# A one-core block: the order of the first transfers, the squares of x, and twenty warm-up matmuls

## The reference

```python
def rms_norm(x, w):
    xf = x.astype(jnp.float32)
    return (xf * lax.rsqrt(jnp.mean(xf * xf, axis=-1, keepdims=True) + RMS_EPS)).astype(x.dtype) * w

    u = rms_norm(h, norm_w[i])          # h = x for the first layer
    proj = u @ in_w                     # z | x, B, C | dt
    xbc = jax.nn.silu(causal_depthwise_conv(xbc, conv_w, conv_b))
    dt = jax.nn.softplus(dt_raw + dt_bias)
```

## Time and profile before

| | us |
|---|---|
| median of three runs | 927.24 |
| the profiled execution | 923.9 |
| its span, first to last instruction | 922.1 |
| PE busy | 874.7 (95%) |
| PEld busy | 841.7 (91%) |
| DVE busy | 553.8 (60%) |
| ACT busy | 481.3 (52%) |
| POOL busy | 620.7 (67%) |

### The profile page before, as it was taken

How to read it: one execution, slowest core, us unless ns; L and a number is a source line. 1 busy time by engine, 2 the same in 40 slices (tenths; PEclk the granted TensorE clock), 3 DMA queues, 4 the chain that set the end, 5 groups by cost and what they waited for, 6 DMA issues and landing times.

```text
span 922.1 us, 18225 instructions
## 1 busy us (share of the span) xinstructions
PE 874.7 (95%) x7019; PEld 841.7 (91%) x7019; DVE 553.8 (60%) x1553; ACT 481.3 (52%) x921; POOL 620.7 (67%) x274
## 2 busy tenths in 40 slices
PE   7999899998998799999999997989999999999995
PEld 6999899988997699999999986978999999999995
DVE  5998557773244744445358987666546666651165
ACT  6755555554455366555545465645555444544451
POOL 3899645556886355455869897343586888888980
PEclk9999899999999999999999998999999999999997
DMA  8677532323664334244646565332465666666621
GB/s 322 180 216 219 163 99 90 96 86 112 188 193 134 106 96 133 92 121 129 197 149 195 171 206 184 91 93 69 108 180 155 195 191 189 185 167 182 204 89 47
DMA packets 38534, 138.85 MB, mean 151 GB/s; under 512 B 4272, under 2 KB 4272, under 8 KB 38448
## 3 DMA queue, kind: packets, MB, share of 16 engines
q1 hardware_dynamic: 38448, 137.69, 49.6%
HBM read 136.63 MB, written 1.05 MB: 149 GB/s over the span
## 4 chain that ended last, share of the span: by engine, by line
PE 74%; DVE 6%; POOL 4%; ACT 2%; issue 2%; DVEq 0%; ACTq 0%
PE ps L548 20%; PE ps L549 19%; PE ps L550 19%; POOL wl L509 4%; PE ps L573 1%; PE ps L743 1%; PE ps L745 1%; PE ps L581 1%; PE ps L659 1%; PE ps L765 1%; PE ps L864 1%; DVE qr L1669 1%; ACT wh L980 1%; PE ps L641 1%; PE ps L888 1%
## 5 line engine op out<-in xcount | busy, mean ns | idle before, releaser
L509 POOL TENSOR_TENSOR wl<-raw,wh 128x1024 fp32r<-128x1024 f32 x254 | 609.3, 2420 | 260.5 <-ACT wh L980 260.4
L548 PE MATMUL ps<-uh,wh 128*128 128x256 f32 x1248 | 354.3, 284 | 7.3 <-DVE ul L1476 3.2
L549 PE MATMUL ps<-ul,wh 128*128 128x256 f32 x1248 | 349.7, 280 | 0.0
L550 PE MATMUL ps<-uh,wl 128*128 128x256 f32 x1248 | 349.4, 280 | 0.0
L980 ACT ACTIVATE wh<-raw 128x1024 fp32r<-128x1024 f32 x256 | 263.0, 1054 | 118.9 <-PE ps L550 115.6
L548 PEld LDWEIGHTS ps<-uh,wh 128*128 128x128 f32 x1248 | 236.1, 189 | 12.3 <-DVE ul L1476 3.4
L549 PEld LDWEIGHTS ps<-ul,wh 128*128 128x128 f32 x1248 | 235.9, 189 | 0.0
L550 PEld LDWEIGHTS ps<-uh,wl 128*128 128x128 f32 x1248 | 235.5, 189 | 0.0
L1634 DVE TENSOR_TENSOR h<-ps,h 128x256 f32<-128x256 f32 x32 | 13.6, 424 | 116.8 <-PE ps L550 116.7
L549 PE MATMUL ps<-ffl,wh 128*128 128x256 f32 x176 | 49.3, 280 | 0.0
L548 PE MATMUL ps<-ffh,wh 128*128 128x256 f32 x176 | 49.1, 279 | 0.0
(11 more groups left out here) (360 smaller groups left out, 1785.2 us busy)
## 6 DMA issues: line engine op xcount, KB each, us to landing
raw<-slabs SPq DMA_DIRECT2D x256, 512.0 KB, 3.9
h<-x_fm SPq DMA_DIRECT2D x4, 256.0 KB, 5.9
out_fm<-outb SPq DMA_DIRECT2D x4, 256.0 KB, 2.2
cst<-shape_consts SPq DMA_DIRECT2D x1, 768.0 KB, 8.3
vec<-vectors SPq DMA_DIRECT2D x1, 303.5 KB, 4.0
pin<-p_fm SPq DMA_DIRECT2D x1, 256.0 KB, 4.7
```

The source lines that it names most:

```text
L509: nc.gpsimd.tensor_tensor(wl[:, s % PART_RING, :], raw[:, s % RAW_RING, :], wh[:, s % PART_RING, :].bitcast(f32), ALU.subtract).then_inc(s ...
L548: nc.tensor.matmul(res, w_h, a_h, start=first, stop=False)
L549: nc.tensor.matmul(res, w_h, a_l, start=False, stop=False)
L550: ins = nc.tensor.matmul(res, w_l, a_h, start=False, stop=last)
```

## The change

It has four parts.
- SP issues the first two tiles of x, then vector columns 0 to 7 with a semaphore of their own (`gain_in`), then slab 0. The other six tiles of x stand before slab 1. The constants and the rest of the vector columns (`vec_in`) stand before slab 3.
- ACT makes `uh` of tiles 0 and 1 before the high part of slab 0, and `uh` of tiles 2 to 7 after it. It squares only tiles 0 to 3, between the high parts of slabs 1 and 2. DVE makes `ul` of tiles 0 and 1 before the low part of slab 0, and squares tiles 4 to 7 as products (`first_sq`) after the low part of slab 1. The additions go: PE sums over the 8 squared tiles in PSUM (`first_sum`), 16 matmuls of one column instead of 2.
- DVE makes the low part of three slabs instead of two; POOL begins with slab 3.
- 20 warm-up matmuls instead of 10.

```diff
-FIRST_SLABS = 2
-WARM_UP = 10
+FIRST_SLABS = 3
+FIRST_GAINS, FIRST_SQUARES = 8, 4
+WARM_UP = 20
...
-        n_ssm = Norm(tile_of(h), 8, DM, "norm0", lambda k: (f"x_in{k // LOAD_TILES}", 16), **into_u)
+        n_ssm = Norm(tile_of(h), 8, DM, "norm0", lambda k: (f"x_in{k // LOAD_TILES}", 16), tile_of(uh), tile_of(ul),
+                     late=True, squared=False)
+        Norm.squares += FIRST_SQUARES
...
-                if s == 1:
-                    sp_.dma_start(vec[:], vec_dram).then_inc(sem("vec_in"), 16)
-                    for i in range(0, KD, LOAD_TILES):
+                if s == 0:
+                    sp_.dma_start(h[:, 0:LOAD_TILES, :], x_dram[:, 0:LOAD_TILES, :]).then_inc(sem("x_in0"), 16)
+                    sp_.dma_start(vec[:, 0:FIRST_GAINS], vec_dram[:, 0:FIRST_GAINS]).then_inc(sem("gain_in"), 16)
+                elif s == 1:
+                    for i in range(LOAD_TILES, KD, LOAD_TILES):
                         sp_.dma_start(h[:, i:i + LOAD_TILES, :], x_dram[:, i:i + LOAD_TILES, :])\
                             .then_inc(sem(f"x_in{i // LOAD_TILES}"), 16)
-                elif s == 2:
+                elif s == 3:
                     sp_.dma_start(cst[:], const_dram).then_inc(sem("const_in"), 16)
+                    sp_.dma_start(vec[:, FIRST_GAINS:], vec_dram[:, FIRST_GAINS:]).then_inc(sem("vec_in"), 16)
...
+            def first_sum():
+
+                for b in range(TB):
+                    for k in range(KD):
+                        if b == 0 and k < FIRST_SQUARES:
+                            wait(pe, "norm_sq", n_ssm.t0 + k + 1)
+                        elif b == 0:
+                            pe.wait_ge(sem("first_sq"), k - FIRST_SQUARES + 1)
+                        ins = nc.tensor.matmul(PS_M[:, b:b + 1], n_ssm.sqb(k)[:, b * P:(b + 1) * P], ones[:, 0:1],
+                                               start=k == 0, stop=k == KD - 1)
+                ins.then_inc(sem("norm_sum"), 1)
...
                 if c == 0:
-                    norm_sum(n_ssm)
+                    first_sum()
...
+            act.wait_ge(sem("gain_in"), 16)
+            for k in range(2):
+                high(n_ssm, k)
             feed_slabs(0)
-            act.wait_ge(sem("vec_in"), 16)
-            for k in range(4):
-                high(n_ssm, k)
-            for k in range(2):
-                square(n_ssm, k)
-            for k in range(4, KD):
+            for k in range(2, KD):
                 high(n_ssm, k)
             feed_slabs(1)
-            for k in range(2, 5):
+            for k in range(FIRST_SQUARES):
                 square(n_ssm, k)
             feed_slabs(2)
-            for k in range(5, KD):
-                square(n_ssm, k)
             feed("dt")
             act.wait_ge(sem("const_in"), 16)
+            act.wait_ge(sem("vec_in"), 16)
...
+            for k in range(2):
+                late_low(n_ssm, k)
             first_slab(0)
-            for k in range(KD):
+            for k in range(2, KD):
                 late_low(n_ssm, k)
             first_slab(1)
-            for k in range(KD):
-                add_square(n_ssm, k)
+            for k in range(FIRST_SQUARES, KD):
+                tt(n_ssm.sqb(k), h[:, k, :], h[:, k, :], ALU.mult).then_inc(sem("first_sq"), 1)
+            first_slab(2)
             dve.wait_ge(sem("vec_in"), 16)
```

## The result

The changed kernel took 930.34 us in the median of 22 runs (926.55 to 932.88), the kernel before 928.34 in 22 runs of its own (its first three gave 927.24). The ratio is 1.0024, with a 95% interval of 1.0015 to 1.0032: 2.2 us slower, between 1.4 and 3.0. The forecast was a shift of +0.4 on 927.24, with a range to 930.2. The sign was right, the size was not, and the level on which I put the shift was 1.1 us low. The measured median lies 0.14 us above the range. That it fell outside at all is owed to the level as much as to the shift: set on 928.34, the same range would have held it.

The account below looks back on a forecast made before the run. The prediction took TensorE's unbroken projections from xbc3's start at 25.53 us as the bound. It summed -1.33 (xbc0) - 0.63 (sqsum) + 2.99 (sums) - 0.61 (pause) = +0.42 us, so 927.24 + 0.4 = 927.6 us, range 925.0 to 930.2.

Parts of the forecast that it names:

- the level: Whole kernel's time before the change: the shift of +0.4 was added to 927.24 us, the median of three runs.
- The bound, the start of xbc3 at 25.53: First stage on TensorE: projections run unbroken from xbc3's start at 25.53, so the change is worth that moment's shift.
- Transfers: slab 1 at 9.8: Opening transfers: with less queued ahead, slab 1 lands at about 9.8 us (9.45 to 10.44) instead of 10.44.
- xbc0 1.33 earlier: First projection, xbc0: starts at 12.15 instead of 13.48, after slab 1's earlier landing and high and low parts; -1.33 us.
- The wait for sqsum, 0.63: Between xbc0's end and the sums: TensorE's wait from 16.41 to 17.04 goes with the seven additions; -0.63 us.
- the pause, 0.61: Before xbc3: TensorE's pause from 24.92 to 25.53 closes because L1502 hardly waits for GpSimd; -0.61 us.
- The sums at 3.45: Between xbc0 and xbc1: 32 sum instructions take 3.45 us against 0.46 before; +2.99 us.
- The small-matmul rival: Sums before xbc1: the 32 instructions take at most 0.92 us instead of 3.45; total 925.1 us; chance 0.10.
- So xbc2 starts 4.48 later: From xbc1 to xbc2: the gap stays 4.48 us as before, so xbc2 starts at 23.01 after xbc1 at 18.53.
- the right mechanism among the rivals, at 0.08: Sums before xbc1: nearly empty array drops the clock to 1.2 GHz, sums take twice as long; +3.45, 931.1 us; chance 0.08.
- The warm-up at nothing: Start of TensorE's work: the longer warm-up counts 0 us, since only dt ran then and is through by 12.15.
- The step sum: Start of xbc3: -1.33 (xbc0), -0.63 (sqsum), +2.99 (sums), -0.61 (pause) give +0.42 us.

Follow-up runs that it names:

- squares alone: Kernel before with only the shared squares, 16 one-column sums and three slabs' low parts on DVE; old transfers, 10 warm-ups: median 930.92 us, ratio 1.0030.
- wider first columns: Changed kernel with a first vector transfer of 128 columns instead of 8: 932.93 us in one execution.
- wide sums: Changed kernel with each of the 16 sum matmuls multiplying by 128 columns of ones instead of one: median 927.78 us, ratio 0.9999.
- e7: Changed kernel with all 16 one-column sum matmuls done twice, 64 instructions: 936.88 us in one execution.
- e8: Changed kernel with a first vector transfer of 128 columns (64 KB) instead of 8 (4 KB): 932.93 us in one execution.
- e14: Third profile of the changed kernel with two one-column sum matmuls behind each step of xbc0 instead of all after it: 933.27 us.
- e13: Changed kernel, unaltered, profiled a second time: 929.66 us.
- e1: Changed kernel with 128 columns of ones instead of one in each sum matmul: median 927.78 us, ratio 0.9999.
- interleaved kernel: Changed kernel with two one-column sum matmuls behind each step of xbc0 instead of all after it: median 929.9 us, ratio 1.0048.
- e2: First profile of the changed kernel with sum matmuls placed between the steps of xbc0: 927.59 us; median of seven runs 929.9.
- e11: Second profile of the changed kernel with sum matmuls placed between the steps of xbc0: 926.51 us.

## Why the prediction was wrong, by its steps

- **The bound, the start of xbc3 at 25.53:** held. Its two executions have it at 25.53 and 25.55. But it is not all that an execution's time hangs on: what follows varies by 3 us, in part by the pace, 1.6 us a stretch.
- **Transfers: slab 1 at 9.8.** It landed at 3.52 + 6.6 = 10.1. The gain of 0.6 was 0.3 or nothing, since the old transfers had slab 1 at 9.94 in one execution and at 10.4 to 10.5 in two (squares alone).
- **xbc0 1.33 earlier.** 0.92 (12.56); in thirteen executions with this order and twenty warm-ups, 12.03 to 12.79. The larger part of it was ACT's order and not the transfers (squares alone).
- **The wait for sqsum, 0.63, and the pause, 0.61:** both went. L1502 took 0.34.
- **The sums at 3.45:** 3.49. The small-matmul rival is out. Of the two rules of the Trainium skill ("TensorE: Matmul & The Clock Gate", back-to-back issue gap and LDWEIGHTS) the one on the weights agrees: 0.109 us each.
- **"So xbc2 starts 4.48 later":** this step failed. It took xbc1 at full clock for certain. In the changed kernel's two executions it was 6.01 and 4.47, with wider first columns 6.74, and the clock made the difference. I had the right mechanism among the rivals, at 0.08, with the price of a fall inside the sums only (+3.45). What the runs show in its place: a fall in four of five executions with these sums, of 1.5 us behind them in three and of 3.1 inside them in one. Against it I had only the 1.70-us stretch at 205.67, half as long, and I let it speak for 3.45.
- **The warm-up at nothing:** the medians can't tell it from nothing, but the reason was wrong. In the profile with ten, dt at half clock held xbc0 up until 14.1, 1.6 us later than with twenty.
- **The level:** 927.24 was the median of three runs; 22 gave 928.34.

The step sum by what was measured, for the first profile: -0.92 - 0.63 + 3.03 - 0.61 + 1.53 (clock) = +2.40, the 27.93 - 25.53 of the trace. Without a fall it is +0.87, and the second profile has +0.89 (26.42). The measured +2.2 lies between. That the sign came out right is partly luck: with the fall taken away by columns, the wide sums' ratio is 0.9999, no loss that the runs can tell.

Shown by an experiment that changes nothing else: the thin columns cost 2.3 us, by eleven runs against 22, and the profiles show the clock as the way in which they do (wide sums). Left open: what decides whether and where the clock falls in an execution, and what sets the pace of 0.113 or 0.118.

## What to carry to other kernels

A matmul with one column costs TensorE the load of its weights: count 0.1 us for each float32 instruction, not the column. Here 3.5 us of such matmuls were enough for the clock to fall from 2.4 to 1.2 GHz in four executions of five, so that the dense work behind them ran at half speed; 1.7 us of them never did it in three. If they must be long, give them columns that cost nothing, or halve them, and don't thin dense work out with them. Before summing on one profile, see whether its own time is near the median of its kernel, and find out why not.

## What the runs showed of the hardware that I had not expected

- The granted clock fell with TensorE busy without a pause: after 3.9 us of one-column sums and the start of xbc1 (changed), inside the sums (e7, e8), and in mixed work of which half is one-column (e14, for 10.2 us). It did not in one profile of the changed kernel (e13), nor in the one with 128 columns in the same instructions (e1).
- Columns are free under a load of weights: 32 instructions take 3.49 us with 1 column and 3.49 with 128; 16 rounded ones 1.70 and 1.73.
- At full granted clock dense projections run at one of two paces, 0.113 or 0.118 us a matmul, for stretches of 40 us and more (31.5 to 71.9 and 210 to 257 us in the first profile of the kernel before, neither in its second; 26 to 72 us in two profiles of the interleaved kernel, e2 and e11). A stretch is worth 1.6 us, some seven tenths of the whole effect of this change.
